# Delta heads: the 2x2 base of the inverse from the gram on VectorE, qkd products on GpSimd, one convolution tap on ScalarE

## The reference

```python
qkv = silu(centred_dwconv(p, conv_w))               # 5 taps
q, k = l2_norm(q), l2_norm(k)
# one chain, in chunks of 64 tokens, gc = cumulative log decay within the chunk
decay = exp(where(lower, gc[..., :, None] - gc[..., None, :], -inf))
a = where(strict, (k * beta) @ k.T * decay, 0.0)
t_inv = triangular_solve(eye + a, eye)              # (I + a)^-1
u, w = t_inv @ (v * beta), t_inv @ (k * beta * exp(gc))
qk = q @ k.T * decay
# per chunk: v_new = u - w @ s;  o = (q * exp(gc)) @ s + qk @ v_new;  s = s * gl + k_dec.T @ v_new
```

## Time and profile before

| what | us |
|---|---|
| median of 3 runs | 1957.88 |
| the three runs | 1957.53, 1957.88, 1962.0 |
| the profiled execution | 1963.0 |
| its span (first to last instruction) | 1961.2 |
| TensorE busy in the span | 1838.9 (94%) |
| VectorE busy | 1036.4 (53%) |
| ScalarE busy | 614.9 (31%) |
| GpSimd busy | 81.6 (4%) |
| mean granted TensorE clock, as a share of full speed | 0.970 |

### The profile page before, as it was taken

One profiled execution on the slowest core, in us unless ns is written; L12 is line 12 of the kernel. 1 busy time (PEld: TensorE's weight loads), 2 busy tenths in 40 slices (PEclk: granted clock), 3 DMA queues, 4 the chain that ended last, 5 costly groups with the idle time before them and its releaser, 6 DMA issues. The chain is left out here.

```text
span 1961.2 us, 38867 instructions
## 1 busy us (share of the span) xinstructions
PE 1838.9 (94%) x16056; PEld 1322.6 (67%) x16056; DVE 1036.4 (53%) x2067; ACT 614.9 (31%) x1318; POOL 81.6 (4%) x59
## 2 busy tenths in 40 slices
PE   6999999999999999998988799988999899999997
PEld 2566666666666666543675687767785687888886
DVE  3567676767676766312136468875556692321101
ACT  2335344445444453302024143243332540100000
POOL 1000000001010100000000000010000000000000
PEclk8999999999999999999999899989999899999999
DMA  9121313111011112022220341322102223443434
GB/s 349 77 99 43 110 44 109 54 67 44 24 45 34 35 44 78 1 97 106 91 86 20 127 190 66 129 103 82 35 34 98 86 87 129 152 170 130 171 151 150
DMA packets 52237, 183.63 MB, mean 94 GB/s; under 512 B 5856, under 2 KB 9312, under 8 KB 51808
## 3 DMA queue, kind: packets, MB, share of 16 engines
q1 hardware_dynamic: 52064, 181.18, 25.4%
HBM read 179.06 MB, written 2.10 MB: 92 GB/s over the span
## 5 line engine op out<-in xcount | busy, mean ns | idle before, releaser
L878 PE MATMUL banks<-u,w_ring 128*128 128x512 f32 x768 | 368.3, 605 | 4.7 <-DVE u L711 4.7
L379 PE MATMUL banks<-u,w_ring 128*128 128x256 f32 x1248 | 304.0, 392 | 8.4 <-PEq L188 8.4
L379 PEld LDWEIGHTS banks<-u,w_ring 128*128 128x128 f32 x1248 | 234.2, 195 | 48.7 <-issue 18.6
L878 PEld LDWEIGHTS banks<-u,w_ring 128*128 128x128 f32 x768 | 138.5, 192 | 115.0 <-issue 104.0
L403 PE MATMUL banks<-u,w_ring 128*128 128x256 f32 x640 | 138.4, 379 | 0.5 <-PEq L188 0.5
L403 PEld LDWEIGHTS banks<-u,w_ring 128*128 128x128 f32 x640 | 121.5, 190 | 17.3 <-issue 0.8
L910 DVE SCALAR_TENSOR_TENSOR acc<-raw,hc,acc 128x512 f32<-128x512 f32 x128 | 107.8, 842 | 4.6
L3575 PE MATMUL banks<-gated,w_ring 128*128 128x512 f32 (+1 forms) x288 | 96.8, 498 | 1.8 <-PEq L188 1.8
L3575 PEld LDWEIGHTS banks<-gated,w_ring 128*128 128x128 f32 x288 | 54.6, 190 | 44.1 <-issue 40.8
L3575 PE MATMUL banks<-ffn,w_ring 128*128 128x256 f32 x352 | 79.1, 389 | 3.0 <-PEq L188 3.0
L3575 PEld LDWEIGHTS banks<-ffn,w_ring 128*128 128x128 f32 x352 | 68.9, 196 | 13.2 <-issue 3.3
(11 more groups left out here) (532 smaller groups left out, 2989.6 us busy)
## 6 DMA issues: line engine op xcount, KB each, us to landing
w_ring<-in_w SPq DMA_DIRECT2D x289, 512.0 KB, 5.7
gated<-in_ada SPq DMA_DIRECT2D x32, 512.0 KB, 4.6
h<-in_h SPq DMA_DIRECT2D x2, 2048.0 KB, 10.4
hold<-h SPq DMA_DIRECT2D x1, 1024.0 KB, 5.2
h<-hold SPq DMA_DIRECT2D x1, 1024.0 KB, 9.4
out<-u SPq DMA_DIRECT2D x8, 128.0 KB, 2.0
const_base<-in_const SPq DMA_DIRECT2D x1, 896.0 KB, 12.3
const_part<-in_const SPq DMA_DIRECT2D x1, 640.0 KB, 4.2
```

The source lines that it names most:

```text
L379: mm = self.nc.tensor.matmul(place, self.st.chunk(g % 2, slot)[:, P * k:P * k + P], self.src(k), start=(k == 0), stop=(k == KT - 1))
L878: mm = nc.tensor.matmul(self.places[m % len(self.places)][:, :], (st.slot(m) if g is None else st.chunk(g % 2, m))[:, P * k:P * k + P], u[ ...
```

## The change

The pair entries of a (level 0 of the inverse) are no longer read from transposed `a_t`. VectorE masks the gram itself with the pair masks of both directions (`cells`), and since the gram is symmetric the wanted entry stands in place. Its weight is beta of the other row of the pair, times exp(g) of the later one: TensorE swaps the betas within pairs with four 64x64 products (`swap`), VectorE multiplies them with the new column EA = exp(g) (`weights`), and `base` makes identity minus gram times weight. All of that is done at the end of the head before (and for head 0 in the opening), so the 16 transposes, the masked blocks and the subtractions at the start of a head are gone. `border` of level 1 now waits for the chains itself, and VectorE's order at the border is changed. The four qkd products move to GpSimd, behind the scaling of the values, and ScalarE waits for them in step 0 of the scan. The first tap of tile 3's convolution moves to ScalarE. One product of the next head moves from behind the output transposes to before them (REST), and in heads 4 to 7 one moves from behind the low products to before them. The opening makes EA with one more exp and two more copies. `prod` moves from `dec` to `spare`; the semaphore sets grow from 60 to 66.

```diff
--- before.py
+++ after.py
...
             front.rows(pe, 3)
+            front.swap(pe)
             front.products(pe, DN_GROUP * KT - front.at)
...
+            front.cells(dve, link)
+            front.weights(dve, link)
+            front.base(dve, link, 0)
+            front.base(dve, link, 1)
             for c in range(4):
                 front.chain(dve, link, c)
...
-        prod = dec[:, :, :].rearrange("p a x -> p (a x)").rearrange("p (d s t e) -> p d s t e", d=2, s=2, t=TT)
+        prod = spare[:, 0:2, :].rearrange("p a x -> p (a x)").rearrange("p (d s t e) -> p d s t e", d=2, s=2, t=TT)
...
+        pair_w = state[:, 1, 0:4 * TT].rearrange("p (d t j) -> p d t j", d=2, j=2)
+        base_masks = CS("lev_b0", 2 * LEVELS).rearrange("p (d n e) -> p d n e", d=2, e=P)[:, :, 0, 0:64]
+        pair_gram = qkd[:, 3, :].rearrange("p (d t e) -> p d t e", d=2, e=64)
...
+                if m == 3:
+                    act.wait_ge(self.s["taps"], self.up("taps", 1))
+                    link(nc.scalar.activation(acc[:, m, :].rearrange("p (a t) -> p a t", a=2), raw[:, m, :, 0:SEQ], ACT.Copy,
+                                              scale=hc[:, 5 * m:5 * m + 1]), self.s["tapped"])
...
             def conv(self, dve, link, m):
                 dve.wait_ge(self.s["raw_out"], self.up("raw_out", m + 1))
                 out = acc[:, m, :].rearrange("p (a t) -> p a t", a=2)
-                link(nc.vector.tensor_scalar(out, raw[:, m, :, 0:SEQ], hc[:, 5 * m:5 * m + 1], None, ALU.mult))
+                if m == 3:
+                    dve.wait_ge(self.s["tapped"], self.up("tapped", 1))
+                else:
+                    link(nc.vector.tensor_scalar(out, raw[:, m, :, 0:SEQ], hc[:, 5 * m:5 * m + 1], None, ALU.mult))
...
+            def swap(self, pe):
+
+                pe.wait_ge(self.s["normed"], self.up("normed", 1))
+                for d in range(2):
+                    for hb in range(2):
+                        beta = self.hs[half(hb), 4 * TT * BETA:4 * TT * BETA + 4 * TT].rearrange("p (j d t) -> p d j t", j=2, d=2)[:, d]
+                        mm = nc.tensor.matmul(bank[2][half(hb), 16 + 8 * d:24 + 8 * d], C(f"lev_{'bf'[d]}0")[half(hb), half(hb)], beta,
+                                              start=True, stop=True)
+                mm.then_inc(self.s["swapped"], 1)
+
+            def cells(self, dve, link):
+
+                dve.wait_ge(self.s["kq_done"], self.up("kq_done", 1))
+                for hb in range(2):
+                    link(nc.vector.tensor_tensor(pair_gram[half(hb)],
+                                                 four(gram)[half(hb), :, half(hb)].unsqueeze(1).to_broadcast([64, 2, TT, 64]),
+                                                 base_masks[half(hb)].unsqueeze(2).to_broadcast([64, 2, TT, 64]), ALU.mult))
+
+            def weights(self, dve, link):
+
+                dve.wait_ge(self.s["swapped"], self.up("swapped", 1))
+                grown = self.hs[:, 4 * TT * EA:4 * TT * EA + 4 * TT].rearrange("p (j d t) -> p d t j", j=2, d=2)
+                link(nc.vector.tensor_tensor(pair_w, bank[2][:, 16:32].rearrange("p (d j t) -> p d t j", d=2, j=2), grown,
+                                             ALU.mult))
+
+            def base(self, dve, link, d):
+
+                mine = inv[:, d].rearrange("p (t j) e -> p t j e", j=2)
+                link(nc.vector.tensor_tensor(mine, pair_gram[:, 1 - d].unsqueeze(2).to_broadcast([P, TT, 2, 64]),
+                                             pair_w[:, d].unsqueeze(3).to_broadcast([P, TT, 2, 64]), ALU.mult))
+                link(nc.vector.tensor_tensor(inv[:, d], eye[:, :].unsqueeze(1).to_broadcast([P, 2 * TT, 64]), inv[:, d], ALU.subtract),
+                     self.s["based"])
...
+                if made:
+                    pool.wait_ge(s["kq_done"], made.up("kq_done", 2))
+                    pool.wait_ge(s["dec_ready"], made.up("dec_ready", 4))
+                for c in range(4):
+                    link(nc.gpsimd.tensor_tensor(qkd[:, c, :], kq[:, :], dec_of[c], ALU.mult), s["qkd_ready"])
...
-                for c in (0, 2, 1, 3):
-                    if made:
-                        pe.wait_ge(s["chained"], made.up("chained", c + 1))
-                        pe.wait_ge(s["dec_ready"], made.up("dec_ready", 3 + c // 2 if c < 3 else 4))
-                        pe.wait_ge(s["o_out"], 2 * n)
-                    for t in range(TT):
-                        mm = nc.tensor.transpose(tile(bank[2 * (c % 2) + c // 2], t), tile(a_t[:, c, :], t), C("ident"))
-                    mm.then_inc(s["a_done"], 1)
...
-                    pe.wait_ge(s["silu"], made.up("silu", 2))
+                    pe.wait_ge(s["silu"], made.up("silu", 3))
+                    pe.wait_ge(s["gate_in"], made.up("gate_in", 1))
                 for t in range(TT):
                     mm = nc.tensor.transpose(tile(bank[6], t), tile(kn, t), C("ident"))
                 mm.then_inc(s["turned"], 1)
-                if made:
-                    pe.wait_ge(s["silu"], made.up("silu", 4))
-                    pe.wait_ge(s["gate_in"], made.up("gate_in", 1))
                 for t in range(TT):
                     mm = nc.tensor.transpose(tile(bank[7], t), tile(y[:, 2, :], t), C("ident"))
                 mm.then_inc(s["turned"], 1)
+                if made:
+                    pe.wait_ge(s["dec_ready"], made.up("dec_ready", 4))
+                    pe.wait_ge(s["o_out"], 2 * n)
+
+                def inverse_ready(lv, d):
+
+                    if lv:
+                        pe.wait_ge(s["t_ready"], due("t_ready", 2 * (lv - 1) + d + 1))
+                    elif made:
+                        pe.wait_ge(s["based"], made.up("based", d + 1))
 
                 quarters = [(t, j, hb) for t in range(TT) for j in range(2) for hb in range(2)]
 
                 def border(lv, d):
 
-                    pe.wait_ge(s["t_ready"], due("t_ready", 2 * (lv - 1) + d + 1))
+                    inverse_ready(lv - 1, d)
+                    if lv == 1 and made:
+                        pe.wait_ge(s["chained"], made.up("chained", 3 + d))
...
-                ahead(LAST)
+                ahead(LAST if n < 4 else 2 * LAST)
...
-                ahead(2 * LAST)
+                ahead(2 * LAST if n < 4 else LAST)
...
                     front.grams(pe)
                     ahead(REST[2])
+                    front.swap(pe)
                     pe.wait_ge(s["kq_done"], front.up("kq_done", 2))
...
+                    if step == 0:
+                        act.wait_ge(s["qkd_ready"], due("qkd_ready", 4))
...
-                if made:
-                    dve.wait_ge(s["kq_done"], made.up("kq_done", 2))
-                for c in range(2):
-                    link(nc.vector.tensor_tensor(qkd[:, c, :], kq[:, :], dec_of[c], ALU.mult), s["qkd_ready"])
-                for d in range(2):
-
-                    dve.wait_ge(s["a_done"], due("a_done", 2 * d + 2))
-                    for hb in range(2):
-                        blocks_a = banks[half(hb), 2 * d:2 * d + 2, :].rearrange("p j (t e) -> p j t e", e=P)[:, :, :, half(hb)]
-                        link(nc.vector.tensor_tensor(by_chain(inv[half(hb), d]), blocks_a, mask(d, 0)[half(hb)], ALU.mult))
-                    mine = inv[:, d]
-                    link(nc.vector.tensor_tensor(mine, eye[:, :].unsqueeze(1).to_broadcast([P, 2 * TT, 64]), mine, ALU.subtract), s["t_ready"])
-                link(nc.vector.tensor_tensor(qkd[:, 2, :], kq[:, :], dec_of[2], ALU.mult), s["qkd_ready"])
                 for lv in range(1, LEVELS - 1):
                     for d in range(2):
-                        dve.wait_ge(s["a_done"], due("a_done", 4 + 2 * (lv - 1) + d + 1))
+                        dve.wait_ge(s["a_done"], due("a_done", 2 * (lv - 1) + d + 1))
                         link(nc.vector.tensor_tensor(prod[:, d], both(sums(2 * d, 256)), mask(d, lv), ALU.mult), s["p_ready"])
...
-                link(nc.vector.tensor_tensor(qkd[:, 3, :], kq[:, :], dec_of[3], ALU.mult), s["qkd_ready"])
...
                     front.conv(dve, link, 3)
+                    front.cells(dve, link)
                     front.chain(dve, link, 0)
+                    front.chain(dve, link, 1)
                     output(0)
-                    front.chain(dve, link, 1)
                     output(1)
+                    front.weights(dve, link)
+                    front.base(dve, link, 0)
+                    front.base(dve, link, 1)
                     front.chain(dve, link, 2)
+                    front.silu(dve, link, 3)
                     front.chain(dve, link, 3)
-                    front.silu(dve, link, 3)
```

More of the change, by code:

```diff
@@ L651, in _ @@
             front.keep(act, link, 1)
+            act.wait_ge(s["g_ready"], 1)
+            link(nc.scalar.activation(ea, lg, ACT.Exp), s["e_ready"])
             act.wait_ge(s["ex"], 1)
@@ L689, in _ @@
             link(nc.vector.tensor_scalar(o_scale, o_source, 0.5, None, ALU.mult))
```

(14 more changed lines are left out.)

25 lines of the change are left out of this document (13 added, 12 removed).

## The result

The changed kernel is slower: a median of 1966.43 us in 13 runs (1959.67 to 1972.0) against 1959.72 us in 13 runs of the kernel before (1954.87 to 1963.97), a ratio of 1.0041 with the interval [1.0029, 1.0054]. The forecast was 1947.1 us with a range up to 1954.0. The profiled execution of the changed kernel took 1971.71 us, against 1963.0 before; its span, 8.7 us longer, is the sum of these parts, taken from the timelines of TensorE.

The account below looks back on a forecast made before the run. TensorE was taken as the bound, busy 91.1 of 92 us in a head. Seven borders gain 13.1 us, the opening loses 2.3, so 10.8 off the 1957.9 us median gives 1947.1 us, range 1942.5 to 1954.

Parts of the forecast that it names:

- From there each level is tiled with PE work as before: From the first update of level 1 in each head's inverse, TensorE's work stays as before, so only its earlier start counts.
- Rival D: TensorE's unexplained 2.28 us stop in head 7 recurs in most runs: 5.3 us less gain, 1952.6; chance 0.15.
- The border: Between two heads: output transposes to first update 14.3 us instead of 16.99, update 1.87 us earlier; seven borders 13.1 us.
- ScalarE's tap: At the border, one added 0.60 us pass on ScalarE before tanh and the output's squaring, taking 0.5 off VectorE.
- the output transposes: On TensorE at the border of heads 1 and 2, they start near 282.3 instead of 281.48.
- One tap stayed held: At the border, GpSimd's output scaling holds VectorE's fourth tap instead of the third; taps end at 282.75 against 282.67.
- The rule on the shared port pair: GpSimd stalls VectorE passes with two SBUF inputs; the levels' passes, one input in PSUM, stay at 0.69 us.
- GpSimd's products: Four qkd passes per head, 0.95 us each, behind the scaling of values; 23 us of cover before the scan, cost zero.
- The opening: Before head 0, VectorE's weights wait for the beta swap, so the first update comes later: loss 2.3 us (1.8 to 2.9).
- The long pause in front of the heads: TensorE pauses 6.8 us in the opening, then runs 3.2 to 5.5 us at half clock, adding 1.6 to 2.7.
- The chances: Odds given for the whole change: 0.74 faster, 0.21 same, 0.05 slower; the forecast itself had 0.62.

Follow-up runs that it names:

- a shift alone in three sizes: Changed kernel with 32, 64 or 96 more TensorE instructions (already fulfilled waits) at the program's start: 1954.28, 1953.29 and 1951.56 us.
- two controls: Changed kernel with the 192 waits behind the delta stage: 1985.47 us; kernel before with the same 192 waits at the start: 1962.80 us.
- 96 more instructions: Changed kernel with 192 already fulfilled waits (96 instructions) at the start of TensorE's program: 1951.56 us, 0.9959 of the kernel before.

## Why the prediction was wrong

**The step that failed** is "From there each level is tiled with PE work as before". The work was the same, its length was not: +21.1 us in the eight heads, against a gain of 11.6 at seven borders and in the scans between them. It came from late instruction blocks and the half clock behind them, a wait of TensorE that the prediction put at nothing. Shown are: that all 91 pauses stand at one number modulo 256 and end 1.2 to 1.7 us behind the end of an instruction packet, that no edge was crossed earlier than that, the gain from a shift alone in three sizes with two controls, and the part of the large loads. With 96 more instructions the delta stage took 707.9 us in the profiled execution, 13.0 less than before; the medians differ by 8.6, against the 10.8 forecast.

**Rival D** had the right kind of event and the wrong size. It took the pause of the earlier trace rows for one that stands in head 7 or doesn't, 5.5 us. The row did show that it begins in the middle of 32 equal products, and a second of the kind, 0.15 us, was in the same trace; the two are whole multiples of 256 records apart. The pauses of heads 0 to 3 were not foreseen by any rival.

**The border** was right: 14.31 us against 14.3, with VectorE's masked product last. Two terms in it were off and stayed small. ScalarE's tap took 0.72 us, not 0.60, and the output transposes came 1.03 us later behind ScalarE's copy of tile 3 (9.03 instead of 8.00), not 0.8; so a head gained 1.66 us in heads 0 to 3, not 1.87, and seven borders 11.6, not 13.1. One tap stayed held, the fourth instead of the third, as forecast. The rule on the shared port pair, which the prediction cites, held again: VectorE's passes with one input in PSUM kept 0.69 us beside five GpSimd passes.

**GpSimd's products** took 1.31 us each, not 0.95: half the pass of 1024 columns was the wrong row, probably because that pass has one broadcast factor and these have two full inputs (no run has the two forms at one size). The Trainium skill, "GPSIMD Engine Reference", section "Elementwise — side-by-side cycle accounting", gives 4497 ns for an add of 2048 columns with two inputs, 1.12 us for 512 as an estimate; that is nearer, and still short. They were hidden all the same: 5.3 us with 23 of cover.

**The opening** cost 2.2 us, against 2.3: the mark of head 0 was 1.1 us later, though the opening itself reached its projections 1.05 us earlier in this execution. The long pause in front of the heads was 7.04 us (forecast 6.8), and the clock was 0.50 behind it for some 4.2 us (charged: 3.2 to 5.5).

**The chances** that the prediction gives to its rivals add up to 0.72 for "faster", not 0.74.

**What stays open.** Why the packet behind the first edge of a head can start 2.45 us late with no transfer near it isn't known, and so which alignment is best can't be said in advance: the three shifts gave 111 to 116 us in heads 0 to 3, and a shift by other sizes was not tried. The end of the span moved too, by 4 to 6 us with the blocks shifted at the start (1123 us behind the delta stage, against 1127.4 after and 1129.4 before). There the cause is another, at least in part: the pauses on "issue" are the same two, 2.8 us in all, but TensorE had 78.0 us at half clock with 96 more instructions against 84.4 after, which is worth 3.2 us. Why is open.

## What to carry to other kernels

Where TensorE runs many small products back to back, count its instructions: one that stops in the middle of a group "on issue", at whole multiples of 256 instructions from other such stops, is waiting for its own program, and inserting or removing some tens of instructions far ahead can be worth more than the change that one is measuring. So measure a small change at two or three alignments before judging it, and keep large loads away from the stretches in which a block of instructions lasts only a few microseconds. Read "the work is the same, so it takes as long" as a term of the sum that needs its own bound.

## What the runs showed of the hardware

- TensorE's program comes in packets of 16.4 KB, 256 instructions. The 91 pauses at the edges, of 0.15 to 4.5 us, in all 14 profiles, ended 2.2 to 3.8 us behind the start of a packet, 1.2 to 1.7 us behind its end. In the inverse, mostly 64x64 float32 products, a block was used up in 3.0 to 4.1 us.
- With 0.6 to 1.0 MB of modulation loads in between, the next packet started 2.5 to 3.2 us behind the edge, and 0.4 to 1.2 us with small ones. The levels of four heads were 16 us longer with the large loads (one profiled execution each).
- 96 instructions that only hold two fulfilled waits took 10.5 us on TensorE, 0.11 us each.
- A pass of 128x512 with two full inputs in SBUF took GpSimd 1.31 us.
